# Three places in a hand-written order: sample convolution behind the first key chunk, gate products behind two evictions, third slab split ahead of the norm's root

## The reference

```python
def even_mixer(xn, h0, conv_buf, attend, w_in, gq, gk, sb_bias, w_conv, b_conv, w_r, b_r, w_i, b_i, lam, w_out):
    q, k, v, xb, gb = jnp.split(xn @ w_in, [W_A, 2 * W_A, 3 * W_A, 3 * W_A + W_B], axis=-1)
    q, k = rmsnorm(q.reshape(b, t, H_A, HD_A), gq), rmsnorm(k.reshape(b, t, H_A, HD_A), gk)
    o_a = attend(q, k, v, sb_bias).reshape(b, t, W_A)          # stick-breaking attention
    xc, new_buf = causal_dwconv(xb, conv_buf, w_conv, b_conv)  # 4 taps
    h, h_last = rglru(xc, h0, w_r, b_r, w_i, b_i, lam)
    return jnp.concatenate([o_a, h * jax.nn.gelu(gb)], axis=-1) @ w_out, k, v, h_last, new_buf

def rglru(xc, h0, w_r, b_r, w_i, b_i, lam):
    r, i = sigmoid(xc @ w_r + b_r), sigmoid(xc @ w_i + b_i)    # per head
    log_a = -C_LRU * r * softplus(-lam)
    a, u = exp(log_a), sqrt(-expm1(2 * log_a)) * (i * xc)
    ...                                                        # h[t] = a[t] * h[t-1] + u[t]
```

## Time and profile before

| | |
|---|---|
| median of 3 runs | 2662.59 us |
| the profiled execution's own time | 2663.94 us |
| its span in the profile | 2662.2 us |
| busy share of TensorE (PE), VectorE (DVE), ScalarE (ACT), GpSimd (POOL) | 98%, 60%, 33%, 43% |
| granted TensorE clock, mean over the span | 0.991 |

### The profile page before, as it was taken

The page is one execution under the profiler, slowest core; times in us unless marked ns, Lnnn a source line. Parts: engine busy times, 40 slices in busy tenths (PEclk is TensorE's granted clock), DMA queues, the critical chain, the costliest instruction groups (busy, mean ns, idle before and its releaser), DMA issues.

```text
span 2662.2 us, 42672 instructions
## 1 busy us (share of the span) xinstructions
PE 2598.7 (98%) x15961; PEld 2427.1 (91%) x15961; DVE 1601.7 (60%) x2183; ACT 868.4 (33%) x1229; POOL 1133.6 (43%) x919
## 2 busy tenths in 40 slices
PE   7999998889999999999999999999999999999999
PEld 6888786589999999999999999999999999999998
DVE  6355556543566666666667544633667777666674
ACT  5465755533222222222222533432222222222221
POOL 3134342215444445555554421344555555444541
PEclk9999998989999999999999999999999999999999
DMA  5101105841211111111111111211111111111112
GB/s 177 50 26 49 43 25 193 269 169 40 64 48 40 47 47 47 47 47 47 44 42 32 52 53 36 56 45 59 48 48 48 47 47 47 42 45 47 47 32 71
DMA packets 208444, 164.10 MB, mean 62 GB/s; under 512 B 9901, under 2 KB 182038, under 8 KB 208334
## 3 DMA queue, kind: packets, MB, share of 16 engines
q1 hardware_dynamic: 207278, 160.35, 19.5%
q10 hardware_dynamic: 576, 2.10, 0.2%
q0 software_dynamic: 480, 0.11, 0.0%
HBM read 147.83 MB, written 14.69 MB: 61 GB/s over the span
## 4 chain that ended last, share of the span: by engine, by line
PE 78%; DVE 0%; ACT 0%; issue 0%; DVEq 0%
PE psum_all L148 50%; PE psum_all L1975 16%; PE psum_all L2449 6%; PE psum_all L1989 2%; PE psum_all L1963 1%; PE psum_all L1965 1%; PE psum_all L2501 0%; PE psum_all L2465 0%; PE psum_all L2489 0%; PE psum_all L2319 0%; PE psum_all L2535 0%; PE psum_all L1643 0%; DVE mixed_odd L2660 0%; ACT operand_hi_a L1748 0%; PE psum_all L2506 0%
## 5 line engine op out<-in xcount | busy, mean ns | idle before, releaser
L108 POOL TENSOR_TENSOR w_lo_part<-w_raw,w_hi_part 128x1024 fp32r<-128x1024 f32 x94 | 227.4, 2420 | 578.1 <-ACT w_hi_part L104 578.1
L2207 DVE TENSOR_TENSOR x_residual<-x_residual,psum_all 128x512 f32<-128x512 f32 (+1 forms) x616 | 449.9, 761 | 19.4
L148 PE MATMUL psum_all<-operand_hi_c,w_hi_part 128*128 128x364 f32 (+1 forms) x1344 | 298.4, 330 | 4.2 <-DVE operand_lo_c L1752 4.2
L148 PE MATMUL psum_all<-operand_hi_a,w_hi_part 128*128 128x364 f32 (+1 forms) x1344 | 297.7, 330 | 0.2 <-DVE operand_lo_a L1752 0.2
L148 PE MATMUL psum_all<-operand_hi_c,w_lo_part 128*128 128x364 f32 (+1 forms) x1344 | 295.9, 328 | 0.0
L148 PE MATMUL psum_all<-operand_lo_c,w_hi_part 128*128 128x364 f32 (+1 forms) x1344 | 295.3, 328 | 0.0
L148 PE MATMUL psum_all<-operand_lo_a,w_hi_part 128*128 128x364 f32 (+1 forms) x1344 | 295.2, 328 | 0.0
L148 PE MATMUL psum_all<-operand_hi_a,w_lo_part 128*128 128x364 f32 (+1 forms) x1344 | 295.1, 328 | 0.0
L113 POOL TENSOR_TENSOR w_lo_part<-w_raw,w_hi_part 128x1024 fp32r<-128x1024 f32 x54 | 131.6, 2438 | 380.9 <-ACT w_hi_part L97 380.8
L2191 DVE TENSOR_TENSOR gate_conv_ffn<-psum_all,gate_conv_ffn 128x1092 f32<-128x1092 f32 x48 | 62.2, 1296 | 347.6 <-PE psum_all L148 347.6
L148 PEld LDWEIGHTS psum_all<-operand_hi_c,w_hi_part 128*128 128x128 f32 x1344 | 233.8, 188 | 7.9 <-issue 4.3
(11 more groups left out here) (352 smaller groups left out, 5043.4 us busy)
## 6 DMA issues: line engine op xcount, KB each, us to landing
w_raw<-in_w_gate_dram SPq DMA_DIRECT2D x48, 512.0 KB, 3.9
w_raw<-in_w_up_dram SPq DMA_DIRECT2D x48, 512.0 KB, 3.9
w_down_raw_ffn<-in_w_down_dram SPq DMA_DIRECT2D x44, 512.0 KB, 4.1
k_pages<-in_cache_k_dram SPq DMA_DIRECT2D x64, 256.0 KB, 3.7
v_pages<-in_cache_v_dram SPq DMA_DIRECT2D x64, 256.0 KB, 5.1
w_raw<-in_w_in_even_dram SPq DMA_DIRECT2D x20, 512.0 KB, 3.9
w_raw<-in_w_in_odd_dram SPq DMA_DIRECT2D x16, 512.0 KB, 4.8
x_spill<-x_residual SPq DMA_DIRECT2D x8, 546.0 KB, 6.3
```

Source lines behind the costliest of these rows:

```text
L108: pool.tensor_tensor(lo, self.raw[:, raw, :], hi.bitcast(F32), ALU.subtract).then_inc(self.s_lo, 1)
L148: mm = pe.matmul(bank[:, c, 0:width(c)], w, x[:, chunk(c)], start=(k == 0 and step == 0), stop=(k == last and step == 2))
L2207: dve.tensor_tensor(dst, dst, src, op).then_inc(self.pair_read, 1)
```

## The change

It touches layer 0's mixer alone, in three ways. The convolution of the sampled tokens becomes an item of its own, ("conv", 2), in slot 5 behind the eviction of ("k", 0) instead of in slot 4 behind the prompt's convolution. ("gain", 0) goes from the end of slot 9 to slot 10, behind the evictions of ("v", 2) and ("g", 1). And of group 0's k slab, the third slab of all, the high part is copied by ScalarE ahead of `roots_act` instead of in slot 3, waiting for the x slab's products (`filled` at 3); its low part on GpSimd keeps its place in that engine's order.

```diff
@@ -465,12 +465,12 @@
     (("x", 2), ("q", 0), ("out", -1)),
     (("q", 1), ("split", "k"), ("conv", 0)),
     (("q", 2), ("conv", 1), ("square", "q")),
-    (("k", 0), ("split", "v"), ("qs", 0), ("qs", 1), ("qs", 2), ("k", 1), ("scale", "q")),
+    (("k", 0), ("conv", 2), ("split", "v"), ("qs", 0), ("qs", 1), ("qs", 2), ("k", 1), ("scale", "q")),
     (("k", 2), ("norm", "q"), ("r", 0), ("i", 0), ("square", "k")),
     (("v", 0), ("split", "g"), ("r", 1), ("i", 1), ("r", 2), ("i", 2)),
     (("v", 1), ("vt", 0), ("ks", 0), ("ks", 1), ("ks", 2), ("scale", "k")),
-    (("g", 0), ("vt", 1), ("norm", "k"), ("decay", 0), ("gain", 0)),
-    (("v", 2), ("split", "x"), ("g", 1), ("kt", 0), ("kt", 1), ("root", 0)),
+    (("g", 0), ("vt", 1), ("norm", "k"), ("decay", 0)),
+    (("v", 2), ("split", "x"), ("g", 1), ("gain", 0), ("kt", 0), ("kt", 1), ("root", 0)),
     (("g", 2), ("vt", 2), ("kt", 2)),
 )
 LANES = 3
@@ -488,7 +488,7 @@
             if kind == "split":
                 if which == "x":
                     group += 1
-                if group > 4 or (group == 4 and which not in "xq") or (group == 0 and which in "xq"):
+                if group > 4 or (group == 4 and which not in "xq") or (group == 0 and which in "xqk"):
                     continue
             elif not 0 <= group < 4:
                 continue
@@ -1139,6 +1139,7 @@
             norm.split_act(act, lambda k: intake.columns_ready(act, k))
             w.split_hi(act, 1, 0, 1)
             norm.squares_act(act)
+            w.split_hi(act, 2, 1, 0, (filled, 3))
             norm.roots_act(act, intake.exp_act)
 
             def sigmoids(u, by_head):
@@ -1338,6 +1339,8 @@
                                            ).then_inc(edged, 1)
                     pool.tensor_tensor(t[:, 0:n - 1], t[:, 0:n - 1], k[:, 1:n], ALU.mult).then_inc(weighted, 1)
 
+            w.split_lo(pool, 2, 0)
+
             for step in range(-1, 4):
                 for slot in slots_of(step):
                     for kind, which, part in in_order(step, slot):
@@ -1408,7 +1411,6 @@
                     return core.par[:, i + 36 + 4 * j:i + 37 + 4 * j]
 
                 bias = core.par[:, i + 32:i + 33]
-                xcs = xc[:, SEQ:SEQ + NS].rearrange("p (s t) -> p s t", t=SLEN)
                 if part == 0:
                     wait_emptied(dve, ("x", 2, i))
                     if i:
@@ -1420,6 +1422,13 @@
                 for j in (1, 0):
                     o.after()
                     o.did(dve.scalar_tensor_tensor(xc[:, :], xb[:, j:j + T], tap(j), xc[:, :], ALU.mult, ALU.add))
+
+            def conv_sample(i):
+                def tap(j):
+                    return core.par[:, i + 36 + 4 * j:i + 37 + 4 * j]
+
+                bias = core.par[:, i + 32:i + 33]
+                xcs = xc[:, SEQ:SEQ + NS].rearrange("p (s t) -> p s t", t=SLEN)
                 o.did(dve.tensor_copy(xs[:, :, 0:3], core.lru_conv0[:, i, :].rearrange("p (s j) -> p s j", j=3)))
                 o.did(dve.tensor_copy(xs[:, :, 3:3 + SLEN],
                                       xb[:, 3 + SEQ:3 + SEQ + NS].rearrange("p (s t) -> p s t", t=SLEN)))
@@ -1539,7 +1548,7 @@
                 if kind in SLABS:
                     evacuate(key)
                 elif kind == "conv":
-                    conv(which, group)
+                    conv(which, group) if which < 2 else conv_sample(group)
                 elif kind == "norm":
                     r = "qk".index(which)
                     buf = kt[group % 2] if r else mix[:, group, :]
```

## The result

| kernel | median, us | range | runs | against before (95% interval) |
|---|---|---|---|---|
| before | 2662.59 | 2661.86 to 2664.24 | 9 | |
| changed | 2670.12 | 2669.19 to 2671.3 | 9 | 1.0027 (1.0018 to 1.0035) |

The change makes the kernel slower by 7.5 us, 0.27% (0.18% to 0.35%). The profiled execution took 2669.64 us with a span of 2667.9 us, so 5.7 us more than the profiled one of before, which was itself 1.35 us over its median. The traces are compared against each other, so 5.7 us is what they have to explain; the other 1.8 us of the medians they cannot.

The account below looks back on a forecast made before the run. TensorE, busy 98% of the span, was taken as the bound, so only its waits and low clock count. The terms -5.1 - 4.1 + 11.2 + 2.55 - 0.3 gave +4.2 us, 2666.8 us, with a range of 2660 to 2672.5.

Parts of the forecast that it names:

- rival 3: TensorE's clock slower than forecast, in the opening and in slot 11 of each step: 2670.6 us; chance 0.23.
- Part A: Opening of step -1: k's second chunk starts near 61.5, not 64.93, at the high clock; -5.1 us.
- Part B: End of step -1: v's and g's evictions go at once and the 2.50 us wait goes; -4.1 us.
- Part C: Steps 0 and 1: slot 11's logits wait 3.5 us longer for the output copy, plus 2.1 of clock each; +11.2 us.
- The meeting: Slot 10, steps 0 to 2: gain's first product waits for GpSimd's split of slab x, taking about 2.9 us.
- Part D: Step 2: gain meets the split and delays the fill of queries, +3.15, with -0.6 for the clock; +2.55 us.
- ScalarE, -0.3: Slot 11: ScalarE's lateness of 0.3 us at the values may go twice; half was taken, -0.3 us.
- Rival 1: Gain does not meet GpSimd's split of slab x in steps 0 to 2: -0.1, or 2662.5 us; chance 0.12.
- Rival 2: Slot 11's logits do not wait for the output copy and the clock stays up: -10.4, or 2652.2 us; chance 0.05.

Follow-up runs that it names:

- run 5: The kernel before with the early split of slab k alone, the sample convolution at its old place: 2663.07 us, 1.0002.
- run 8: The changed kernel with GpSimd's low-part split of slab x cut from 1024 columns to 8 in steps 0 to 2: 2662.84 us, 0.9995.
- run 1: The changed kernel with the gain's products at the new place in step -1 alone, at the old one in steps 0 to 2: 2653.82 us, 0.9965.
- run 3: The kernel before with the early split of slab k and the moved sample convolution, the gain at its old place: 2656.74 us, 0.9977.
- run 4: The kernel before with the moved sample convolution alone: 2658.25 us, 0.9979.
- run 2: The kernel before with the gain's move alone: 2673.92 us, 1.0039.
- run 10: Run 1 with the queries of the cached part filled behind slot 11 of step 2 instead of behind slot 10: 2653.28 us, 0.9961.
- run 11: Run 10 with the last group's recurrence behind g's last eviction in step 2 and the queries behind slot 0 of step 3: 2650.35 us, 0.9946.
- run 7: Run 6 with ScalarE's root moved to the end of slot 11, behind that slot's sigmoids: 2657.64 us, 0.9975.
- run 6: The changed kernel with VectorE's output copy for slot 11 issued ahead of the gain in slot 10 of steps 0 to 2: 2657.63 us, 0.9978.
- run 9: The changed kernel with 6, 6 and 8 dropped matmuls on TensorE ahead of slot 11's logits in steps 0 to 2: 2663.97 us, 1.0003.
- run 12: Run 11 without the early split of slab k: 2647.51 us, 0.9943.

## Why the prediction came out as it did

The forecast was slower by 4.2 us, just inside 0.2%; it is slower by 7.5, on the side to which the chances gave 0.40 and not 0.55. The range held it, the likeliest case didn't reach it, and it lies between the forecast and rival 3. (The upper end of the range, from the terms named for it, is 2662.6 + 9.55 = 2672.1, not 2672.5.)

- **Part A, -5.1: measured -4.8.** Right in its steps: softplus held up for one split (2.37 us, predicted 2.36; the instruction held, L365, has one tensor as its input and not two, as the prediction had it), evictions later by 1.17 (predicted 1.3), k's second chunk at 61.5 with the high clock. L1418 took 0.84 and not 0.6. What the step had wrong was its title: it credited the split with the 1.69 us. Its own working showed that k's second chunk waits for the convolution and the logarithm, not for the first chunk, and run 5 shows it: alone, the split brings nothing.
- **Part B, -4.1: measured -4.17.**
- **Part C, 2 x (3.5 + 2.1) = +11.2: measured 6.10 + 6.04 = +12.1.** The wait was right: the logits start 3.46 us later against the rest (198.85 + 8.99 - 204.38). The meeting was right (2.83 us against 2.9), and run 8 shows that it is GpSimd's. **The term that was mis-sized is the clock**: 2.1 us was taken between 1.6 and 2.7, and it was 6.50 - 3.86 = 2.64 each time, the upper bound, as rival 3 had it. The row for it was at hand: step 2's slot 11 in the earlier trace rows, the same work behind such a wait, had cost 2.7, while the 1.6 came from other work. But neither size is a law. The same wait of 2.62 us cost 1.4 to 1.6 us in runs 1, 3, 4 and 5, and run 2, with the changed kernel's waits, paid 1.94 and 2.26, beside the forecast's 2.1. How near one number comes is partly luck.
- **Part D, +2.55: measured +2.29.** The logits start 419.28 - 413.70 - 2.37 = 3.21 us later against the rest, where 3.15 was forecast (2.37 is the shift carried over from step 1), and the clock was cheaper by 0.92 us (6.54 - 5.62), not 0.6.
- **ScalarE, -0.3: measured -0.78.** It went twice, in full.
- **Behind step 2, 0: measured +1.1.** No step of the prediction looked there. Waits of 1.5, 1.2 and 4.24 us that the change doesn't touch cost 1.66 us more, 1.56 less and 1.0 more clock in the profiled execution. The traces of the other runs, none of which edits these places, take one value or another: the 1.66 us stand in those of runs 8, 10 and 11 and in no other, and behind the wait of 1.2 us the work takes as long as before in run 7, 1.56 us less in run 6, and 3.1 us less in runs 2, 5, 9 and 12. So this is a spread between executions that the forecast left out, and it is not shown to be an effect of the change.
- **Rival 1** (no meeting) is excluded by the 2.83 us. Run 8, where the meeting is taken away, took 2662.84 us where rival 1 said 2662.5. **Rival 2** (no wait for the copy) is excluded by 4.45 us. **Rival 3** (2670.6) was nearest to the time, and half right: the clock of slot 11 in steps 0 and 1, not the opening's, so that it came within 0.5 us of the time is luck.
- What the prediction did not see is that the gain holds up ScalarE as well. It named what is queued behind the gain on VectorE alone. It cost the forecast nothing, since VectorE's wait covered it, but it took about half of what run 6 should have won.

Left open: what decides from one execution to the next how much clock the same wait costs, what the 1.8 us are by which the medians differ more than the traces, and whether GpSimd's split could be put elsewhere in slots 10 and 11, which wasn't tried.

## What to carry to other kernels

A move that helps in the one step where an engine is idle can cost in the steps where the same slot is full: the table of slots is shared by all steps, and 9 us of gain were paid for with 14 until the move was made in step -1 alone. Before work is put later in a queue, list what stands behind it on its own engine and what stands behind its consumer on the next one; here both the output copy and, through the root, the sigmoids were held up. And where TensorE is the bound, a wait costs more than its length: in slot 11 of this kernel those of 2.6 to 6.4 us cost 1.4 to 2.7 us of low clock besides. An edit that is worth 1 or 2 us can't be judged by one trace of each kernel, since the clock of untouched places moved by as much.

## What the runs showed of the hardware

In these traces the price of a wait in clock does not grow with its length. From logits to L957 of slot 11, with 3.86 us at the high clock:

| wait ahead, us | from logits to L957 | extra |
|---|---|---|
| 0.40 (before, step 0) | 3.86 | 0 |
| 2.62 (before, step 2) | 6.54 | 2.68 |
| 2.62 (runs 1, 3, 4, 5, step 2) | 5.37, 5.41, 5.41, 5.30 | 1.44 to 1.55 |
| 2.91 (run 8, step 0) | 5.41 | 1.55 |
| 4.45, 4.47 (changed, steps 0 and 1) | 6.50, 6.50 | 2.64 |
| 4.46, 4.47 (run 2, steps 0 and 1) | 5.80, 6.12 | 1.94, 2.26 |
| 4.89 (run 8, step 2) | 6.10 | 2.24 |
| 6.43 (changed and run 2, step 2) | 5.62, 5.40 | 1.76, 1.54 |

The granted clock came back at different points of the same work. Shorter waits are not safe either: behind that of 1.5 us in the cached part the next 14 us of work ran at 1.00 in the traces of before and run 1, and at 0.89, 1.6 us longer, in those of the changed kernel and run 10; behind that of 1.2 us the same work took 13.6 us in one trace and 10.5 in another (before, run 12); and the wait of 4.24 us ahead of the next block cost 1.0 us more in one trace than in the other. A forecast can take a mean, but a spread of 1.2 us for each wait belongs in its range.

In these traces GpSimd's hold on VectorE does not depend on the size of VectorE's instruction: a product of 1092 elements lost 1.5 us, and one of four elements with a single tensor as its input lost 2.2 (L365, 2.37 us for 0.16 to 0.17 elsewhere). It waits to the end of GpSimd's instruction, whatever that still has to do.
